# The delta layer's sums of squares as rows of four column strips, its output norm spread from rows of tokens, and the q, k, v panels taken before the weights' residual

## The reference, cut to what matters

```python
def l2norm(x):
    xf = x.astype(jnp.float32)
    return xf * lax.rsqrt(jnp.sum(xf * xf, axis=-1, keepdims=True) + EPS)

    qkv = jax.nn.silu(causal_dwconv(qkv, conv_w))           # four taps
    q = l2norm(q.reshape(B, Lp, H, Dh)) * (Dh ** -0.5)
    k = l2norm(k.reshape(B, Lp, H, Dh))
    ...
    _, O = lax.scan(step, S0, (...))                        # state 128 x 128 per head
    O = rmsnorm(O, o_gain) * jax.nn.silu(og.reshape(B, Lp, H, Dh).astype(jnp.float32))
    return (O.reshape(B, Lp, DN_HD).astype(h.dtype) @ w_out)[:, pad:]
```

## Time and profile before

| what | us |
|---|---|
| median of 3 runs (2830.24 to 2832.62) | 2831.06 |
| the profiled execution | 2832.84 |
| its span, first to last instruction | 2831.1 |
| PE busy in the span (92%) | 2616.0 |
| DVE, ACT, POOL busy | 1375.5, 965.6, 987.1 |

### The profile page before, as it was taken

One profiled execution on the slowest core, in us unless ns is written; L12 is line 12 of the kernel. 1 busy time (PEld: TensorE's weight loads), 2 busy tenths in 40 slices (PEclk: granted clock), 3 DMA queues, 4 the chain that ended last, 5 costly groups with the idle time before them and its releaser, 6 DMA issues.

```text
span 2831.1 us, 46056 instructions
## 1 busy us (share of the span) xinstructions
PE 2616.0 (92%) x19938; PEld 2350.9 (83%) x19938; DVE 1375.5 (49%) x2139; ACT 965.6 (34%) x1515; POOL 987.1 (35%) x585
## 2 busy tenths in 40 slices
PE   6999977899999989999999999989999999999997
PEld 4777766678888777887989999888888888999997
DVE  3545447363535444444264555455453434636464
ACT  4233343232323433333333323443232223333232
POOL 0653434634444322221534444500001213444444
PEclk8999988999999999999999999999899998999998
DMA  6532220323333211111213333312111002233221
GB/s 193 148 103 64 58 67 1 104 75 97 95 92 89 68 45 38 46 45 38 83 53 90 90 87 88 91 45 60 37 33 31 20 28 61 68 90 90 87 84 62
DMA packets 379931, 201.37 MB, mean 71 GB/s; under 512 B 6465, under 2 KB 377153, under 8 KB 379729
## 3 DMA queue, kind: packets, MB, share of 16 engines
q1 hardware_dynamic: 379728, 198.42, 24.8%
HBM read 196.30 MB, written 2.10 MB: 70 GB/s over the span
## 4 chain that ended last, share of the span: by engine, by line
PE 57%; DVE 22%; ACT 11%; issue 5%; POOL 3%; DMA 1%; SPq 0%; POOLq 0%; ACTq 0%; DVEq 0%
PE ps L640 39%; DVE t_ffy L2740 7%; ACT t_wh L608 5%; DVE t_ffy L2743 2%; DVE t_atq L2540 2%; ACT t_ffy L2647 2%; PE ps L2357 1%; POOL t_wl L618 1%; DVE t_ffy L2749 1%; PE ps L2956 1%; PE ps L2296 1%; PE ps L2330 1%; PE ps L2975 1%; PE ps L484 1%; PE ps L1038 1%
## 5 line engine op out<-in xcount | busy, mean ns | idle before, releaser
L618 POOL TENSOR_TENSOR t_wl<-t_raw,t_wh 128x1024 fp32r<-128x1024 f32 (+2 forms) x268 | 610.4, 2279 | 1010.8 <-ACT t_wh L608 1010.8
L608 ACT ACTIVATE t_wh<-t_raw 128x1024 fp32r<-128x1024 f32 (+2 forms) x323 | 327.7, 1015 | 608.6 <-PE ps L640 571.1
L640 PE MATMUL ps<-t_hh,t_wh 128*128 128x264 f32 (+2 forms) x2048 | 478.3, 313 | 12.6 <-ACT t_wh L608 4.9
L640 PE MATMUL ps<-t_hh,t_wl 128*128 128x264 f32 (+2 forms) x2048 | 453.8, 301 | 3.1 <-POOL t_wl L618 2.6
L640 PE MATMUL ps<-t_hl,t_wh 128*128 128x264 f32 (+2 forms) x2048 | 451.3, 302 | 0.0
L640 PEld LDWEIGHTS ps<-t_hh,t_wh 128*128 128x128 f32 x2048 | 329.1, 195 | 33.2 <-issue 14.9
L640 PEld LDWEIGHTS ps<-t_hh,t_wl 128*128 128x128 f32 x2048 | 328.9, 194 | 18.4 <-issue 5.0
L640 PEld LDWEIGHTS ps<-t_hl,t_wh 128*128 128x128 f32 x2048 | 327.8, 194 | 9.4 <-issue 1.5
L640 PE MATMUL ps<-t_fhh,t_wh 128*128 128x264 f32 (+1 forms) x1040 | 281.9, 325 | 7.2 <-DVE t_fhl L1690 5.6
L640 PE MATMUL ps<-t_fhh,t_wl 128*128 128x264 f32 (+1 forms) x1040 | 280.6, 324 | 4.6 <-POOL t_wl L618 4.5
L2740 DVE SCALAR_TENSOR_TENSOR t_ffy<-t_ffp,t_vec,t_ffy 128x528 f32<-128x528 f32 x88 | 216.8, 2463 | 130.6 <-ACT t_ffy L2647 130.6
...
## 6 DMA issues: line engine op xcount, KB each, us to landing
...
```

Source lines behind the costliest of these rows:

```text
L608: ac.activation(wh[slot_of[j]][:, 0:kc, :], raw[r % NRAW][:, 0:kc, :], ACT.Copy).then_inc(up("wh_cut", "cut", j), 1)
L618: eng.tensor_tensor(wl[slot_of[j]][:, 0:kc, :], raw[r % NRAW][:, 0:kc, :], wh[slot_of[j]][:, 0:kc, :].bitcast(F), SUB).then_inc(up(name, " ...
L640: ins = pe.matmul(ps[bank_of(j, i)][:, 0:tn], wt[slot][:, k, :], a[:, k, t0:t0 + tn], start=first, stop=last)
```

## The change

(1) In the stage "qkv" the take of panel j stands before the cut of panel j+2. (2) `l2_sums` goes. The squares of q and k go into `ogT`, which is free until the "og" panels; once per group `l2_rows` sums four heads at once, each matmul with a 128 x 32 block of ones into its own 32 partitions of a bank, 16 matmuls of 264 columns. ACT copies the rows of k, `l2_turn` transposes them (5 matmuls), DVE picks the columns; DVE scales the rows of q into `nqT`. Both stand at ticks (`token_sums`), ahead of the workers, and not behind a panel. The first take of "og" waits for the sums of group 1, through `until` in the plan and a semaphore. (3) `fsum` uses strips too (8 matmuls per group). `froot` now takes root and reciprocal of a whole 128 x 528 tile and splits it into a high and a low part; `fmul` spreads with 4 matmuls of 264 columns per head, a 32 x 128 block of 1/32 as stationary operand.

```diff
@@ taken
             if ended:
                 put("warm")
-            else:
+            elif panels[j].stage != "qkv":
                 cut_to(j + 2, j)
             put("take", j)
             for sem in read_by(j):
                 sig.mark(sem, "take", j)
+            if not ended:
+                cut_to(j + 2, j)
@@ gemm, ahead of taken(...)
+                while until and not until():
+                    tick()
@@ then_qkv
-            if x == 2:
-                put_off(j, "l2_sums", h, banks=1)
+        def token_sums(G):
+            while G not in SQUARED:
+                yield 0
+            put("l2_rows", G, banks=4)
+            SUMMED.add(G)
+            yield ALONE
+            put("l2_turn", G, banks=2)
+            put("knorm", G)
+            NORMED.add(G)
+            yield 1
@@ finish
             for e in range(4):
                 put("fsq", G, e)
+            yield 1
+            yield 1
+            put("fsum", G, banks=2)
+            put("froot", G)
+            for _ in range(5):
                 yield 1
-                put("fsum", G, e, banks=1)
-            yield 1
-            put("froot", G)
-            yield 1
...
-        behind.extend([worker(0), worker(1), first_end])
+        behind.extend([token_sums(0), token_sums(1), worker(0), worker(1), first_end])
...
-        gemm(("og",), then_og, keep=0, every=6)
+        gemm(("og",), then_og, keep=0, every=6, until=lambda: 1 in SUMMED)
@@ delta_tensor
+            def l2_rows(G):
+                bs = bank("l2_rows", G)
+                for x in range(2):
+                    for b, (t0, tn) in zip(bs[2 * x:2 * x + 2], HALF):
+                        held(b)
+                        for e in range(4):
+                            w.wait_ge(s.squared, at("squared", "dsilu", 4 * G + e, x))
+                            ins = pe.matmul(ps[b][32 * e:32 * e + 32, 0:tn], C("ones", 128, 32),
+                                            squares_of(x, e)[:, t0:t0 + tn], start=True, stop=True)
...
+            def l2_turn(G):
...
+                w.wait_ge(s.copied, at("copied", "l2_rows", G))
+                for n, (t0, tn) in enumerate(TILES):
+                    o = ps[b][:, 128 * n - 128:128 * n] if n else ps[b2][0:NM, 0:128]
+                    ins = pe.transpose(o, krow[:, t0:t0 + tn], C("ident"))
...
+                    for i, x in enumerate(froots[G][1:]):
+                        ins = pe.matmul(ps[b][:, 0:tn], share[p32, 0:1].to_broadcast([32, 128]), x[p32, t0:t0 + tn],
+                                        start=i == 0, stop=i == 1)
@@ delta_scalar, froot
+                ac.activation(r, r, ACT.Sqrt).then_inc(up("rooted", "froot", G), 1)
+                w.wait_ge(s.inverted, at("inverted", "froot", G))
+                ac.activation(high, r, ACT.Copy).then_inc(up("hi_set", "froot", G), 1)
@@ delta_vector, froot
-                dv.reciprocal(fs[:, G], fs[:, G]).then_inc(up("inverted", "froot", G), 1)
+                dv.reciprocal(r, r).then_inc(up("inverted", "froot", G), 1)
+                w.wait_ge(s.inverted, at("inverted", "froot", G))
+                w.wait_ge(s.hi_set, at("hi_set", "froot", G))
+                dv.tensor_tensor(low, r, high.bitcast(F), SUB).then_inc(up("lo_dve", "froot", G), 1)
```

More of the change, by code:

```diff
@@ L353, in taken, with gemm @@
             cut_to(j + 3 if ended and j + 3 in THIRD else j + 2, j)
-        def gemm(stages, then=None, keep=1, every=0, feed=None, tail=False, group=0, two=False):
+        def gemm(stages, then=None, keep=1, every=0, feed=None, tail=False, group=0, two=False, until=None):
             js = [j for j, p in enumerate(panels) if p.stage in stages and p.group == group]
@@ L1819, in program @@
         s1 = ExitStack()
+        with ExitStack() as st:
+            spent = [sbt(st, f"dspent{i}", [128, 8, L], R) for i in range(2)][1]
         dk = sbt(s1, "dk", [128, 8, L])
@@ L2068, in program @@
             "uh": "multiplied scaled/y scaled", "ui": "multiplied scaled", "uj": "multiplied h_run copied",
[L2069 removed]
+            "fsq": "squared", "fsum": "summed scaled", "froot": "rooted inverted hi_set lo_dve", "fmul": "spread normed",
         })
@@ new lines, in fsum @@
+            def fsum(G):
+                for b, (t0, tn) in zip(bank("fsum", G), HALF):
+                    held(b)
+                    for e in range(4):
+                        w.wait_ge(s.squared, at("squared", "fsq", G, e))
+                        ins = pe.matmul(ps[b][32 * e:32 * e + 32, 0:tn], C("ones", 128, 32), dk[:, 4 * G + e, t0:t0 + tn],
+                                        start=True, stop=True)
+                    free[b] = [(s.scaled, at("scaled", "fsum", G))]
+                ins.then_inc(up("summed", "fsum", G), 1)
```

160 lines of the change are left out of this document (77 added, 83 removed).

## The result

The changed kernel took 2786.62 us (median of 5 runs, 2782.24 to 2787.45) against 2830.87 for the kernel before (5 runs, 2826.62 to 2832.62): ratio 0.984, 95% interval 0.9826 to 0.9855. The forecast was 2809 with a range of 2797 to 2823: the direction was right, the gain twice as large, 44 us for 22. The profiled execution took 2786.62 as well.

The account below looks back on a forecast made before the run. PE was busy 92% of the span, but a loop of ACT and DVE paced group 0. Terms -11.6 - 13.8 + 2.5 + 1.5 + 2.5 + 2.7 - 5 - 1.2 = -22.4 gave 2809 us, range 2797 to 2823.

Parts of the forecast that it names:

- Group 0, -11.6: Group 0's qkv panels: with the take before the residual, PE's 5.85 us per panel sets the pace, -11.6 us.
- PE's work: PE's matmuls from 1941 to 2333: sums and spreads removed, strips, transposes and shorter spreads added, net -13.8 us.
- a rival, +9: Clock rival: each of three new waits throws PE back to 1.2 GHz for some microseconds, +9, 2818 us; 12%.
- (a): At l2_rows(0), early in group 1: waits of 2.7 and 3.9 against 5.1 saved at the first unit, net +1.5 us.
- (b): At l2_rows(1), behind the last k panel: PE waits for taps, silu and square, +2.5 us, between 0 and 4.
- (c): At froot(0): root and long reciprocal hold DVE, so PE waits at a ug, +2.7 us, between 0 and 6.
- Waits that shrink, -5: Beside group 1: units' DVE steps queue behind 2.3 us instead of 3.9 in 12 places, -5 us, between 0 and -12.
- `finish(1)`, -1.2: In finish(1): the chain ends 2.4 us earlier, but panels behind it start at half clock, net -1.2 us.
- DVE as the pace: Rival: DVE sets the pace beside group 1 and "og"; half of 13.8 and the 5 are lost, 2821 us; 10%.
- the late residual: Rival: with the take first, each residual ends 0.77 us later and PE waits for it, 2837 us; 4%.
- strips that don't overlap: Rival: the 48 strip matmuls of two records take 37 instead of 6.4 us, 2840 us; 2%.
- Waits that are covered: Rival: ticks slide, ACT catches up and (a) to (c) cost nothing, 11.8 us less, 2797 us; 8%.

Follow-up runs that it names:

- order_only: The kernel before with only the take moved ahead of the cut in the stage qkv: 2803.27 us, ratio 0.9925.
- no_reciprocal: The changed kernel with both reciprocals in froot replaced by a multiplication with 0.5 (output norm not computed): 2782.52 us, ratio 0.9852.
- order_group0: The changed kernel with the take ahead of the cut in group 0 alone, the cut first again in group 1: 2801.46 us, ratio 0.9921.
- sums_only: The changed kernel with the cut ahead of the take again in the stage qkv, sums and output norm as changed: 2819.06 us, ratio 0.9984.
- cut_beside: The changed kernel with group 1's cut of panel j+2 put a tick later, behind the first tap: 2793.87 us, ratio 0.9871.
- fill_finish: The changed kernel with unread matmuls, 16 and 48, in the two places where PE is idle in finish(1): 2785.19 us, ratio 0.9865.

## Why the prediction was wrong, point by point

**Group 0, -11.6: right.** Its last panel ends on PE at 1919.0, before at 1941.5; from the layer's first cut (1857.2 and 1848.1) that is -13.4, of which 1.7 is a start with 10.2 us at low clock where there were 13.7. The second profile, with 13.7, gives -12.0. PE is gapless as forecast. The cuts are 5.17 and 5.85 apart where the loop was put at 5.3 and 5.93.

**PE's work: right.** -13.8 behind 1941, three sums of 2.3 in group 0 and 7.7 in `finish(1)` make -28.4; the table shows 431.2 and 429.2 before, 401.4 and 401.3 now. Strips and transposes took their 2.19 and 1.10 us.

**The rest, by stretch.** The sum's terms split into idle time and clock, against the mean of two profiles each, in us:

| stretch | idle, forecast | idle, measured | clock, forecast | clock, measured |
|---|---|---|---|---|
| group 0 (-11.6 less 6.9 of work) | -4.7 | -2.7 | 0 | -2.6 |
| beside group 1 (+1.5 + 2.5 - 5) | -1.0 | -7.0 | 0 | -11.1 |
| "og" (+2.7) | +2.7 | +0.1 | 0 | -0.9 |
| "do" 0 and `finish(1)` (+2.5; -1.2 plus 7.7 of work) | +7.8 | +8.0 | +1.2 | +4.3 |
| layer | +4.8 | -1.6 | +1.2 | -10.3 |

Clock is half of the time at 1.2 GHz. The work came out as forecast (-28.4 and -28.9), so the error of 18 us is in these two columns, and 17 of it lies beside group 1.

**The step that failed: the clock beside group 1, which the sum put at nothing.** The time at 1.2 GHz there falls from 34.1 us to 17.1 and 6.8, worth 8.5 and 13.7 us; in order_only alone it falls to 20.5. In the sum the clock stands only in `finish(1)`. Elsewhere it was left to a rival, +9 for the three new waits, with "the shrinking waits free as much" against it. So the two were taken to cancel at best, and a gain by the clock had no place in the forecast.

**New waits, +1.5, +2.5, +2.7: the second step, too high.** (a) At `l2_rows(0)` PE did not wait at all (2.7 forecast), since ACT had caught up; ahead of the transposes it waited 3.1 and 1.9 us (3.9); the first unit's wait for its exponentials, 5.1 and 6.5 in the second profile, is gone as forecast. Together -2.0 and -4.6 in place of +1.5. (b) The wait for `l2_rows(1)` didn't come. There is one of 2.6 us five microseconds ahead of it, but that is a tap of 2.33 us beside POOL's residual of the first "og" panel, and 1.7 of it was there before. (c) `froot(0)` cost 2.6, which is gone in no_reciprocal; but the idle time of "og" is 7.3 before and 7.7 and 7.1 now, since other waits of its units went, four for `t_dY` with 5.0 us among them.

**Waits that shrink, -5: about right.** Besides the exponentials, the waits beside group 1 were 9.5 us before, in both profiles, most of them for DVE:

```profile
PE ps L2970 <- DVE t_dY L3293: 3.8, 2, 2.1
PE ps L2956 <- DVE t_dT L3301: 2.4, 2, 1.6
PE ps L2975 <- DVE t_dY L3293: 1.6, 1, 1.6
...
```

Now, besides the one ahead of the transposes, they are 5.7: -3.8. The mechanism was the right one, the queue on DVE in which high part, residual, take and scaling stood before a unit's step. That order_group0 shows 10.9 us for the order alone is no contradiction: it has the sums in their new place, with more of the units beside group 1 (in the windows of the stretch 2197 matmuls, 1953 in the kernel before), so the old order costs more there. 12 places times 1.6 us less of queue is 19, so about half is felt.

**What low clock a gap brings stays open.** The runs show that the order takes low clock away: 34.1 to 20.5 us beside group 1 on the old sums, 23.9 to 17.1 and 6.8 on the new ones. They give no price per us of idle time. sums_only has more idle time there than the kernel before (19.9 for 14.6 and 16.0) and less low clock (24.8 for 34.1), and cut_beside has 17.4 idle and 10.2 low.

Of the Trainium skill ("TensorE: Matmul & The Clock Gate", Part 1: The HAM clock gate) the prediction said that by its rule every idle spell speaks against the change. fill_finish agrees with the rule (1.00 in place of 0.66 with the gaps filled); its sign here was the other one: beside group 1 the change closes more idle time than it opens.

**`finish(1)`, -1.2:** -2.5 at the panels behind it, of which 1.0 is the chain (23.6 for 24.6). The other 1.5 goes with the clock, and the other way round than forecast: before, the panels behind the last subtraction still had 3.4 us at 1.2 GHz, and now they have none. The strips took 3.56 us at low clock, not 1.0, and end 2.0 us behind the last square and not 1.0, which is most of what the chain lacks of its 2.4; the long reciprocal is as expected.

**The rivals.** DVE as the pace, the late residual and strips that don't overlap did not occur: no PE wait for a residual is among those listed. Waits that are covered was true in part: 5 to 7 of its 11.8 us.

Open is also why the changed kernel's layer takes 481.9 or 474.9 with the same instructions; the profiles show 10.3 us less at low clock and 1.7 less idle, not what decides it. That a shorter queue would gain more was not shown: no run beat the changed kernel beyond the spread of its own executions.
